# A parallel-head encoder layer on one core: GELU and gate loads waited for differently, dots and GpSimd's low halves placed differently

## The reference

```python
s = jnp.einsum('thpd,hpnd->thpn', q, subkeys)          # 8 heads, 2 sides, 128 keys
sv, si = lax.top_k(s, K)                               # K = 16 per side
comb = (sv[:, :, 0, :, None] + sv[:, :, 1, None, :]).reshape(T, PEER_HEADS, K * K)
cs, ci = lax.top_k(comb, K)
idx = ia * PEER_NKEYS + ib                             # 16 of 16384 experts per head
g = jax.nn.softmax(cs, axis=-1)
a = jnp.einsum('td,thkd->thk', xb, u_tab[eb])
w = gb * jax.nn.gelu(a, approximate=False)
out = jnp.einsum('thk,thkd->td', w, v_tab[eb])
```

## Time and profile before

| | us |
|---|---|
| median of 3 runs | 1334.58 (1333.9 to 1334.58) |
| the profiled execution | 1335.88 |
| its span, first to last instruction | 1334.1 |
| TensorE busy | 1282.7 (96% of the span) |
| VectorE busy | 1146.9 (86%) |
| GpSimd busy | 720.5 (54%) |
| ScalarE busy | 690.7 (52%) |

### The profile page before, as it was taken

How to read it: one execution, slowest core, us unless ns; L and a number is a source line. 1 busy time by engine, 2 the same in 40 slices (tenths; PEclk the granted TensorE clock), 3 DMA queues, 4 the chain that set the end, 5 groups by cost and what they waited for, 6 DMA issues and landing times.

```text
span 1334.1 us, 22547 instructions
## 1 busy us (share of the span) xinstructions
PE 1282.7 (96%) x7713; PEld 714.5 (54%) x7713; DVE 1146.9 (86%) x2410; ACT 690.7 (52%) x961; POOL 720.5 (54%) x411
## 2 busy tenths in 40 slices
PE   6999999999988999999998999999799999999997
PEld 3554555456655677777764555555344444444444
DVE  8866388899985899999976989889799989898997
ACT  5652654466664788888843343433333334443342
POOL 4741333456784477778743656657574646455502
PEclk9999999999999999999998999999899999999999
DMA  7232422266998699999999999999999999999952
GB/s 298 96 111 64 138 84 79 95 224 206 310 359 286 222 371 398 397 400 392 396 407 357 356 385 365 361 369 365 349 400 402 402 402 402 397 402 401 397 199 102
DMA packets 130469, 405.03 MB, mean 304 GB/s; under 512 B 12512, under 2 KB 48608, under 8 KB 128224
## 3 DMA queue, kind: packets, MB, share of 16 engines
q1 hardware_dynamic: 88928, 253.21, 51.6%
q0 software_dynamic: 41472, 151.01, 29.3%
HBM read 359.09 MB, written 44.56 MB: 303 GB/s over the span
## 4 chain that ended last, share of the span: by engine, by line
PE 70%; DVE 17%; issue 6%; DMA 4%; ACT 2%; POOL 1%; DVEq 0%; SPq 0%; ACTq 0%; POOLq 0%
PE bank L778 34%; PE bank L766 8%; PE bank L768 8%; PE bank L767 8%; PE bank L1043 2%; DVE area L1699 2%; DVE area L1690 2%; DVE area L1692 2%; DMA area<-gates_scratch 2%; PE bank L985 2%; PE bank L987 2%; PE bank L793 2%; DVE area L1696 1%; DVE area L1687 1%; DMA gates_scratch<-area 1%
## 5 line engine op out<-in xcount | busy, mean ns | idle before, releaser
L778 PE MATMUL bank<-cut,area 128*128 128x512 f16 x2208 | 486.3, 381 | 15.5 <-DVE area L1928 15.5
L766 PE MATMUL bank<-hT,cut 128*128 128x352 f16 (+1 forms) x1216 | 394.3, 324 | 12.8 <-POOL cut L635 9.2
L768 PE MATMUL bank<-hT,cut 128*128 128x352 f16 (+1 forms) x1216 | 394.3, 324 | 0.0
L767 PE MATMUL bank<-hT,cut 128*128 128x352 f16 (+1 forms) x1216 | 394.2, 324 | 0.0
L778 PEld LDWEIGHTS bank<-cut,area 128*128 128x128 f16 x2208 | 216.8, 98 | 276.1 <-DVE area L1928 16.4
L1074 ACT ACTIVATE cut<-raw 128x1024 f16<-128x1024 f32 x214 | 223.1, 1055 | 222.5 <-DMA raw<-tiles_dram 180.4
L1460 DVE SCALAR_TENSOR_TENSOR cut<-raw,cut 128x1024 f16<-128x1024 f32 x214 | 269.6, 1261 | 55.5 <-ACT cut L1074 50.4
L635 POOL TENSOR_TENSOR cut<-raw,cut 128x1024 f16<-128x1024 f32 x80 | 169.6, 2136 | 154.7 <-DVE window_word L1705 93.0
L766 PEld LDWEIGHTS bank<-hT,cut 128*128 128x128 f16 x1216 | 119.4, 98 | 90.1 <-issue 12.0
L643 POOL DMA_INDIRECT ple_sb<-u_rows_dram,expert_id x64 | 116.1, 1814 | 94.8 <-DVE dots L1666 54.0
L643 POOL DMA_INDIRECT ple_sb<-v_rows_dram,expert_id x64 | 117.6, 1837 | 82.2 <-DVE ple_gate L1935 75.3
(11 more groups left out here) (225 smaller groups left out, 1592.7 us busy)
## 6 DMA issues: line engine op xcount, KB each, us to landing
raw<-tiles_dram SPq DMA_DIRECT2D x298, 512.0 KB, 7.0
gates_scratch<-area SPq DMA_DIRECT2D x12, 2048.0 KB, 10.4
area<-gates_scratch SPq DMA_DIRECT2D x32, 768.0 KB, 12.8
gelu_scratch<-gelu_out SPq DMA_DIRECT2D x88, 192.0 KB, 5.4
area<-gelu_scratch SPq DMA_DIRECT2D x22, 768.0 KB, 11.8
norm_rows<-norms_dram SPq DMA_DIRECT2D x3, 1024.0 KB, 8.0
hn<-x_dram SPq DMA_DIRECT2D x4, 512.0 KB, 5.0
out_dram<-hn SPq DMA_DIRECT2D x3, 512.0 KB, 2.7
```

What stands on the lines that cost most here:

```text
L766: nc.tensor.matmul(dst, w[0], hT[:, 0, k, 0:width], start=(k == 0), stop=False)
L767: nc.tensor.matmul(dst, w[0], hT[:, 1, k, 0:width], start=False, stop=False)
L768: last = nc.tensor.matmul(dst, w[1], hT[:, 0, k, 0:width], start=False, stop=(k == KD - 1))
L778: mm = nc.tensor.matmul(bank[:, 2 * tt + h, :], lhs(a)[:, tt * P:(tt + 1) * P], cut[:, t.slot, b, h * HALF:(h + 1) * HALF], start=(first a ...
```

## The change

Five edits:

- `load_gelu`: groups 0 and 1 no longer wait on `weight_done`; from group 2 on the wait is as before.
- Gate group 0 is loaded in the *kept* stage before the last chunk is stored, without the last chunk (11 of 12). ScalarE copies the slice of the last chunk from `gate_chunk` itself behind the fourth kept tile. SP waits for the last store and for this copy (`gates_copied`) ahead of `load_gates(1, 0)`; VectorE waits for the copy ahead of the first weight.
- `DOTS_IN_UNIT`: units 5 to 8 take 4 and 4 dots (the last unit 4 and 8) in place of 0 and 6, 2 and 6, 2 and 6, 2 and 8. `LOWS_IN_WINDOW` moves one tile from window 16 to window 17.
- GpSimd issues early gathers between its low halves (two behind each low half from a window's second on), and counts the dots of the window that is open as done.
- In the gate rounds GpSimd cuts the first tile of a pair, once the one-hot operands of the pair are written; VectorE cuts the second, behind its two dots. ScalarE's scaled cut moves to the first tile with it.

```diff
--- before.py
+++ after.py
@@ -83,8 +83,8 @@
 SELECTION = ((0, 1, 0, TT), (1, 2, 2, 2), (3, 2, 2, 2), (5, 2, 2, 2), (7, 1, 2, 2),
              (1, 2, 0, 2), (3, 2, 0, 2), (5, 2, 0, 2), (7, 1, 0, 2))
 LATTER_HALF = 5
-LOWS_IN_WINDOW = (4, 2, 3, 1, 3, 1, 3, 2, 2, 0, 3, 2, 5, 4, 5, 4, 4, 2, 6)
-DOTS_IN_UNIT = ((0, 0),) * 5 + ((0, 6), (2, 6), (2, 6), (2, 8))
+LOWS_IN_WINDOW = (4, 2, 3, 1, 3, 1, 3, 2, 2, 0, 3, 2, 5, 4, 5, 4, 3, 3, 6)
+DOTS_IN_UNIT = ((0, 0),) * 5 + ((0, 4), (4, 4), (4, 4), (4, 8))
 assert len(LOWS_IN_WINDOW) == 2 * len(SELECTION) + 1 and len(DOTS_IN_UNIT) == len(SELECTION) and sum(LOWS_IN_WINDOW) == POOL_TILES
 U_EARLY = U_TOPK + U_SOFTMAX + U_GATES + U_KEPT
 N_BOTH = N_U - U_EARLY
@@ -414,7 +414,7 @@
         gates_stored = [sem(f"gates_stored{s}") for s in range(2)]
         gates_loaded = [sem(f"gates_loaded{s}") for s in range(2)]
         gelu_loaded = [sem(f"gelu_loaded{s}") for s in range(2)]
-        sparse_w_done = sem("sparse_w_done")
+        sparse_w_done, gates_copied = sem("sparse_w_done"), sem("gates_copied")
         weight_done, weight_hi, weight_lo = sem("weight_done"), sem("weight_hi"), sem("weight_lo")
         experts_done, final_sum, final_done, stored = (sem(n) for n in (
             "experts_done", "final_sum", "final_done", "stored"))
@@ -444,7 +444,7 @@
             def load_gates(group, half):
 
                 first = GG * group + U_EARLY if group < EIGHTS else GG * (group - EIGHTS)
-                chunks = slice(GCH // 2 * half, GCH // 2 * (half + 1))
+                chunks = slice(GCH // 2 * half, GCH // 2 * (half + 1) - (1 if group == 0 and half else 0))
                 at_least(sp, weight_done, GG * (group - 1))
                 sp.dma_start(gates_in[:, group % 2, chunks],
                              gates_dram[chunks, :, first:first + GG, :].rearrange("c p e t -> p c e t")
@@ -452,7 +452,8 @@
 
             def load_gelu(group):
 
-                at_least(sp, weight_done, N_BOTH + VG * (group - 1))
+                if group >= 2:
+                    sp.wait_ge(weight_done, N_BOTH + VG * (group - 1))
                 sp.dma_start(gelu_in[:, group % 2], gelu_dram[group]).then_inc(gelu_loaded[group % 2], 16)
 
             def load_norms(stage):
@@ -522,12 +523,13 @@
             for c in range(U_EARLY - U_KEPT, U_EARLY):
                 load(Tile(T_U + c + LOAD_AHEAD))
                 if c == U_EARLY - U_KEPT + 1:
-                    store_gates(GCH - 1, 1, TD // 4)
-                if c == U_EARLY - U_KEPT + 5:
                     for s in range(2):
-                        sp.wait_ge(gates_stored[s], 16 * (GCH // 2))
+                        sp.wait_ge(gates_stored[s], 16 * (GCH // 2 - s))
                     load_gates(0, 0)
                     load_gates(0, 1)
+                    store_gates(GCH - 1, 1, TD // 4)
+            sp.wait_ge(gates_stored[1], 16 * (GCH // 2))
+            sp.wait_ge(gates_copied, 1)
             load_gates(1, 0)
             for i in range(2):
                 load(Tile(T_BOTH + i + LOAD_AHEAD))
@@ -650,13 +652,17 @@
                 if n:
                     pool.wait_ge(window_open, n + 1)
                     dotted += DOTS_IN_UNIT[(n - 1) // 2][(n - 1) % 2]
-                for _ in range(count):
+                for j in range(count):
                     pool_low(Tile(low))
                     low += 1
+                    if n > 2 * LATTER_HALF and j:
+                        for _ in range(begun, min(begun + 2, EARLY, dotted + EARLY_SLOTS)):
+                            gather(begun)
+                            begun += 1
+                if n == 2 * LATTER_HALF:
+                    pool.wait_ge(ids_done, 1)
                 if n >= 2 * LATTER_HALF:
-                    pool.wait_ge(ids_done, 1)
-                    done = dotted - DOTS_IN_UNIT[(n - 1) // 2][(n - 1) % 2]
-                    for _ in range(begun, min(EARLY, done + EARLY_SLOTS)):
+                    for _ in range(begun, min(EARLY, dotted + EARLY_SLOTS)):
                         gather(begun)
                         begun += 1
             assert begun == EARLY and low == POOL_FIRST + POOL_TILES
@@ -668,7 +674,8 @@
                     pool.wait_ge(gated, TT)
                 gather(n)
             for pair in range(U_GATES // 2):
-                t = Tile(T_U + U_TOPK + U_SOFTMAX + 2 * pair + 1 + SPLIT_AHEAD)
+                t = Tile(T_U + U_TOPK + U_SOFTMAX + 2 * pair + SPLIT_AHEAD)
+                pool.wait_ge(onehot_done, pair + 1)
                 pool.wait_ge(lo_cut, t.n)
                 pool_low(t)
                 for n in range(EARLY + ROW_RING + 2 * pair, EARLY + ROW_RING + 2 * pair + 2):
@@ -1350,7 +1357,7 @@
                     for j in range(4):
                         c = U_TOPK + U_SOFTMAX + 4 * s + j
                         t = Tile(T_U + c + 8 * it)
-                        if j % 2:
+                        if j % 2 == 0:
                             scale_and_split_hi(t.plus(SPLIT_AHEAD), 4 * it + 2 * s + j // 2)
                         else:
                             split_hi(t.plus(SPLIT_AHEAD))
@@ -1373,6 +1380,11 @@
                 t = Tile(T_BOTH - U_KEPT + j)
                 split_hi(t.plus(SPLIT_AHEAD))
                 gelu(t, j % 4, kept=j)
+                if j == 3:
+                    act.wait_ge(gates_stored[0], 16 * (GCH // 2))
+                    act.wait_ge(gates_out, TD // 4)
+                    nc.scalar.activation(gates_in[:, 0, GCH - 1], gate_chunk[:, 1, U_EARLY:U_EARLY + GG, :],
+                                         ACT.Copy).then_inc(gates_copied, 1)
 
             def weight_high(i, slot, last_use):
                 act.wait_ge(weight_done, i + 1)
@@ -1882,16 +1894,16 @@
                         c = U_TOPK + U_SOFTMAX + 4 * s + j
                         if j % 2 == 0:
                             onehots(4 * it + 2 * s + j // 2, j // 2)
+                        dot(EARLY + 8 * it + 4 * s + j)
+                        if j % 2:
                             t = Tile(T_U + c + SPLIT_AHEAD + 8 * it)
                             dve.wait_ge(lo_cut, t.n)
                             split_lo(t)
-                        dot(EARLY + 8 * it + 4 * s + j)
                     if it == 0 and s == 0:
                         weigh_extra()
 
             for it in range(U_GATES // 8):
                 build_gates(it)
-            dve.wait_ge(lo_cut, T_BOTH - U_KEPT + SPLIT_AHEAD)
             for c in range(U_KEPT):
                 split_lo(Tile(T_BOTH - U_KEPT + c + SPLIT_AHEAD))
                 for j in range(KEPT_DOTS * c // U_KEPT, KEPT_DOTS * (c + 1) // U_KEPT):
@@ -1902,6 +1914,8 @@
 
                 group, slot = i // GG, i % RING
                 dve.wait_ge(gates_loaded[group % 2], 32 * (group // 2 + 1))
+                if i == 0:
+                    dve.wait_ge(gates_copied, 1)
                 dve.wait_ge(ready, target)
                 at_least(dve, weight_lo, i - RING + 1)
                 nc.vector.tensor_tensor(
```

## The result

The changed kernel takes 1327.02 us, median of 5 runs (1325.06 to 1329.1); the kernel before, run beside it, 1334.58 (5 runs, 1333.9 to 1337.96). The ratio is 0.9931, 95% interval 0.9915 to 0.9947: 9.2 us faster, 7.1 to 11.3. I had predicted 1312.4, 22.2 faster, with a range of 1302 to 1325. The sign was right, the size wrong by more than half. The profiled execution has a span of 1325.7 us against 1334.1: 8.4 less.

A forecast was written before the change was run, and what follows sets the result against it. TensorE, busy 96% of the span, was taken as the bound, with 33.7 us in reach; 8.4 + 5.7 + 8.4 - 0.3 = 22.2 us off 1335.88 gave 1313.7, adjusted to 1312.4 us, range 1302 to 1325.

The forecast's parts named there:

- windows: Window units and softmax start: dots and early gathers spread out remove row waits and shorten first-tile waits; gain 8.4 us, bounds 4 and 13.
- gate rounds: Gate rounds: one-hots 1.0 us faster but worth nothing; GpSimd's low half comes later in the first round; cost 0.3 us.
- gate group 0: Kept stage: loading gates ahead of the store removes the first weight's 9.2 us wait; gain 5.7 us, bounds 0 and 8.7.
- GELU loads: Start of the late stage: SP no longer blocks on the 32nd weight, so the stall goes; gain 8.4 us, bounds 3 and 10.9.
- I take 3.0 us of new waits in all: Kept stage: new TensorE waits for tiles behind the earlier gate loads, taken off the 8.7 us stretch cost.
- The slack of 2.6: Kept stage, first tile behind the store: 2.6 us to spare between its cut and TensorE's need for it.
- VectorE starves then and asks for no more: Kept stage: up to eight rows may pass the gates, but VectorE then stops asking; new wait bounded by 8.7 us.
- 3.5 is the upper bound of what comes back: Late stage: beyond 7.4 us of free DMA time, 3.5 us must come from tiles' early landing; 2.5 taken as lost.
- My own sign of being wrong: The prediction is wrong if late-stage waits exceed 4 us in sum, or the windows lose more than 8.
- DMA takes it back: Rival: both long stalls let DMA catch up, leaving gains of 3 + 0 from them; 1323.5 us, chance 0.15.
- The rival that the gathers stretch: Windows: gathers between low halves take 2.84 us, not 0.95, making the kernel slower, 1347 us; chance 0.06.
- SP blocked all the same: Late stage: gate group 5's wait for the 32nd weight still blocks SP, so the GELU edit does nothing; 1320.8, chance 0.06.

The follow-up runs named there:

- in large pieces: The changed kernel with gate group 0 read in pieces of 5 and 6 KB a partition, not 1 KB: 0.9906 against the kernel before, 12.5 us faster.
- Eight kept dots fewer: The changed kernel with 4 dots in the kept stage in place of 12, eight more in the stage after: 0.9857 against the kernel before, 19.1 us faster.
- group 5's loads apart: The changed kernel with gate group 5's two loads put behind tiles 206 and 208: 0.9925 against the kernel before, 10.0 us faster.
- the change without one of its parts: The changed kernel with the gate group 0 edit undone, loads behind the store as before: 0.9903 against the kernel before, 12.9 us faster.
- The kernel with both orders: The changed kernel with the last chunk's store later and group 5's gate loads behind tiles 206 and 208: 0.9846 against the kernel before, 1314.0 us.
- the one with five sums later: Changed kernel, last chunk's store later, group 5's gate loads behind tiles 206 and 208, late-stage sums moved back: 0.9832 against the kernel before, 22.4 us faster.

## Why the prediction was wrong, point by point

By the two traces the terms are: windows 8.0 (predicted 8.4), gate rounds -1.1 (-0.3), gate group 0 -2.0 (+5.7), GELU loads 11.4 - 5.5 - 1.7 at the end = 4.2 (+8.4), and -0.7 that no edit explains; 8.4 in sum. The runs of single edits say 6.9, -1.7, -2.3 and 4.1, in sum 7.0, against 9.2 for the whole (7.1 to 11.3).

**The step that failed** is the return in "Gate group 0": "I take 3.0 us of new waits in all". It was 10.9, with the clock behind the wait. I had the parts. 1.44 MB "push it back 3.6": right in kind (in large pieces, where rows gain less from it, the wait was 3.4). The slack of 2.6 was read on TensorE's old timetable, on which the edit alone gave 8.1 us of wait. The rows were the miss. I wrote that while rows are waiting, gates get a quarter, and that eight rows may go first, but put no time to it: eight rows are 4.2 MB, 10 us at 407 GB/s. I relied on "VectorE starves then and asks for no more", and went near the low end. VectorE did starve, from 682.45 to 695.75 us, and GpSimd's last gather before that went out at 682.81; but that is 16 us after the gates' issue, and GpSimd issues gathers as far ahead of VectorE as its slots go. In the stretch 4.76 MB of rows passed, nine of them, 2.6 MB or five more than in the stretch before: 6.4 us. The three numbers make 3.6 + 6.4 - 2.6 = 7.4 us of wait (8.1 and 8.8 seen); this sum is made after the fact. With the spell at half clock behind the wait the cost is 10.9, more than the old stall's (8.7). So both the rate and the number of rows were in the prediction, and their product was missing. Eight kept dots fewer ended the wait.

I also read the term as a wait that goes and some bytes that come, and did not look at the 2 MB store in the same place. It could go out 21 us later (689.04 in place of 667.97), once group 1's gates and the weights were moved too. All this together gave 9.6 us; what the store's part is was not measured.

**GELU loads.** Right: SP's gap went, the 10.9 of the stretch were won (11.4), the next wait in SP's list did no harm. Mis-sized: "The other 3.5 must come out of how early tiles land ... 3.5 is the upper bound of what comes back", and I took 2.5. It was 5.5 by the end of the table and 1.7 more behind it, nearly all of it the last tile's wait. So the bound of 3.5 was wrong itself, and not in this kernel alone: 5.7 + 0.5 with the GELU edit alone, 3.9 + 0.4 with group 5's loads apart. For one thing it took the reserve as common to all tiles, but tile 206 stood behind 1.5 MB of gates and waited alone, and a granted clock of 0.93 over 938 to 962 us came with it. For another, by an estimate, the sum lacks a term: five groups of 12.6 MB at the 396 to 400 GB/s that DMA moved behind 1000 us take 157.5 to 159 us, 2.5 to 4 more than TensorE's 155. How the 7.2 us divide between the two isn't shown. My own sign of being wrong, late waits of over 4 us in sum, came: 3.4 + 1.6. The rival "DMA takes it back" (1323.5, chance 0.15) was the nearest to what happened.

**Windows, dots and gathers.** Right in mechanism, and in size in this trace, 8.0 for 8.4. Twelve kernels have this edit; between the same tiles four of their traces win 8.0 us and eight win 6.3, so some luck is in the 8.0 (the last section shows why). VectorE has no wait for rows in the last window, GpSimd's gathers between low halves take 0.96, not 2.84:

```profile
376.48 0.96 POOL L645 DMA_INDIRECT norm_rows<-u_rows_dram,area  x1
...
392.17 0.96 POOL L645 DMA_INDIRECT area<-u_rows_dram,area  x1 [0.16 <-issue]
```

The first-tile waits are at most 2.0, as forecast. The rival that the gathers stretch is out, and the softmax's 3.7 us wait is gone.

**Gate rounds.** Right that the faster one-hot brings nothing (durations in ns, least, median, most, and first and last start):

```profile
L1885 DVE TENSOR_TENSOR ple_gate<-iota_oh_sb,area x24: 2281/2284/2293, 446.0 to 649.6; 128x4096 f16<-128x4096 f16 x24
```

2.28 us in place of 3.27 (medians of 24 rounds), and a round is 8.95 us as before. The first round costs 1.1, the upper part of my 0 to 1.3: TensorE waits 0.9 for that low half. I took 0.3.

**SP blocked all the same, slower by stretched gathers**: neither happened.

**The range** ended at 1325, near the case that returned most (1323.5), in which gate group 0 gave 0 and the GELU loads 3. The result lies 2 us beyond. The bound of 0 came from a new wait as long as the old one's cost, 8.7, and left out the clock behind the new wait.

## What to carry to other kernels

When a load is put ahead of another, ask what shares the DMA engines with it and how much that other queue has outstanding: small pieces ahead of a tile let the other queue's bytes pass, and the tile pays for both. A wait removed in a stretch where DMA is at its rate comes back. Here it came first at the tile with the least reserve and, once that tile was helped, as several short waits behind it; look for that tile, and for a transfer in the same queue that can go later. And price a term by undoing it: here the change without one of its parts was faster than with it.

## What the runs showed of the hardware that I had not expected

Issuing a DMA can take SP long when small pieces are ahead of it. The 2 MB store took 0.43 us to issue before, 7.73 behind the gates in pieces of 1 KB (5.31 and 4.39 in two other kernels with them, gate group 0 alone and 4 kept dots), and again 0.43 behind the same bytes in pieces of 5 and 6 KB:

```profile
668.97 0.96 SPq L451 DMA_DIRECT2D area<-gates_scratch  x2
669.97 0.43 SPq L513 DMA_DIRECT2D gates_scratch<-area  x1
671.95 24.69 SPq L436 DMA_DIRECT2D raw<-tiles_dram  x6
```

So tile 138 was issued 3.8 us earlier there; it was behind gates and store in its queue in both, and the rows above give no sign that this helped it to land.

A few short waits can cost less than their sum in one. The kernel with both orders has two of its four waits, 3.1 us in sum and up to 1.8 each, in this stretch (columns as in the earlier trace rows), and its granted clock stays at 1.00, or 2.4 GHz:

```profile
975.00:1100.00 125.00, 121.88 (x565) 54.95 (x563) 114.25 (x135) 47.59 (x64) 65.07 (x41) 1.00 1.02 396
```

Behind the one wait of 3.1 us in the changed kernel the mean is 0.93 over 24 us, behind that of 8.8 us 0.78 over 23. By the table the wait of 3.1 us cost 5.0.

A wait of one length can cost the clock or not. In all twelve kernels with the window edit TensorE waits 2.0 us for the same low half near 398 us. In four the clock stays at full speed, in eight a spell at half clock follows, which is worth the 1.7 us between 8.0 and 6.3. From 395 to 405 us, the changed kernel, then the one with five sums later:

```profile
395.00:405.00 10.00, 8.00 (x54) 5.05 (x53) 9.84 (x29) 6.54 (x8) 8.57 (x5) 1.00 0.96 324
395.00:405.00 10.00, 8.01 (x43) 4.59 (x42) 9.85 (x29) 5.84 (x7) 8.41 (x4) 0.83 0.98 342
```

What decides it no run here shows.
